# GpSimd makes the low parts of the squares, and VectorE and ScalarE share the rounding of y, in the first pass of an output stage

## The chip, the cores and the metric

One Trainium2 chip, one core, one launch. The metric is the device time of the whole kernel in microseconds. Three runs of the kernel before gave 2103.11 us in the median (2101.9 to 2104.24). All tensors lie in one core's memory; nothing is shared with other cores.

## The reference

The kernel computes two blocks in a row on a sequence of 1024 tokens with 1024 features, in float32: a gated delta net and then a block that mixes a differential attention with an mLSTM. The change lies at the seam, in the end of the first block:

```
o = rms_norm(o, norm_w) * silu(z)          # o, z: 1024 tokens x 16 heads x 128
y = o.reshape(t, 16 * 128) @ w_out         # w_out: 2048 x 1024
x = x + gate * y
x = rms_norm(x, final_g)
```

The mean in the first rms_norm is taken over the 128 features of each head.

## The kernel before

Matrix products of float32 are made from parts that TensorE multiplies fast. Each operand a is split into a high part, a rounded to the type fp32r, and a low part, a minus the high part, again rounded to fp32r. A product is three matmuls: high x high, high x low, low x high. So every operand costs one rounding copy and one subtraction on other engines before TensorE can start on it. Sums over partitions (for the norm) are products with a matrix of ones; the ones are exact, so such a sum takes two matmuls, one for the high and one for the low part.

Data lie transposed: 128 features on the partitions, 1024 tokens in the columns. A tile "of a head" is 128x1024.

The function `stage_out` computes the code above. It is written as one program for each engine, with the order of the instructions in the source and semaphores between engines; no planner orders it. The output has 8 channels of 128 features, and PSUM holds 6 banks of 512 columns for them, so the product is made in three passes over the 16 heads, with 3, 3 and 2 channels (`CH_PASS`). The list `steps` has 48 entries (pass q, head n). In the first pass (q is 0) the heads are normalised as well, and y is kept for the other passes as `y(0, n)` (high) and `y(1, n)` (low). These lie in three tensors (h_hi, m_hi, y2_hi and the same with lo), which is why the same line appears with several names in the profile. The parts of the squares, `sq_hi` and `sq_lo`, are two slots at the end of y2_hi and y2_lo, and show as y_hi and y_lo.

For head n in the first pass:

- SyncE loads o (`ob`), z (`zb`) and the rows of w_out (`m_raw`), each a few heads ahead; ob and zb have three slots, the weights two.
- ScalarE makes the square of o (L1257, into `sq`, two slots) and its high part (L1259). The subtraction that makes the low part is on VectorE (L1421, function `low_square`).
- TensorE sums the squares (L1315, L1316, four matmuls, function `sums`). The sums of head n+2 stand in the middle of head n: after the second of the three channels, which is after 12 of its 18 matmuls (L1352 to L1354).
- ScalarE turns the sums into 1/rms: two Ln from PSUM (L1272) and an Exp (L1275, `rinv`).
- VectorE multiplies z by o and by norm_w ("gated", L1414, in place in zb) and then by rinv ("mult", L1440).
- ScalarE makes the high part of y (L1279); VectorE subtracts and makes the low part (L1446). TensorE's head n waits for this low part.
- VectorE splits the weights (L1405 cast and L1407 subtraction, function `split`).

VectorE's order for head n is: mult(n), split(n), low_square(n+2), low y(n), gated(n+1). ScalarE's is: Ln(n), Exp(n), Square(n+2), high square(n+2), high y(n). GpSimd has no program in this stage; it works in the stages before and after, in element-wise products and sums (L608, L618, L627, L1742).

The second and third pass need only the weights' splits, and draining PSUM (L1382), from VectorE.

Of the kernel before, what the change touches and what calls it, by code (L numbers as in the profile page):

```python
# [22 lines left out]
F32 = mybir.dt.float32  # L23
F32R = mybir.dt.float32r
ALU = mybir.AluOpType
ACT = mybir.ActivationFunctionType
# [10 lines left out]
V_HEADS = 16  # L37
# [1105 lines left out]
def stage_out(nc, io, keep, own):  # L1143

    if True:
# [14 lines left out]
        zb = sb("zb", [P, 3, T])  # L1160
        sq = sb("sq3", [P, 2, T])
# [17 lines left out]
        def y(part, n):  # L1179

            low, middle, high = ((h_hi, next_hi, y2_hi), (h_lo, next_lo, y2_lo))[part]
            if n < KD:
                return low[:, n, :]
            return middle[:, n - KD, :] if n < KD + 2 else high[:, n - KD - 2, :]
# [52 lines left out]
        def scalar(act):  # L1237
            def squares(k):

                act.wait_ge(both_set, 5)  # L1240
                act.wait_ge(bank_used, 2 * (k + 1))
                for r in range(2):
                    if 2 <= k < KD - 1:
                        act.wait_ge(added, 2 * (k - 2) + r + 1)
                    elif k < 2:
                        act.wait_ge(ylo_done, V_HEADS)
                        act.wait_ge(ss_done, V_HEADS)
                    dst = total[:, r, :] if k == 0 else zb[:, r, :] if k == KD - 1 else sq[:, r, :]
                    nc.scalar.activation(dst, x1[:, k, :], ACT.Square,
                                         scale=(1.0 if r else both[:, k:k + 1])).then_inc(sq2, 1)  # L1250

            nc.scalar.preload_act_table_set(EXP_LN)
            def square(n):
                act.wait_ge(o_in[n % 3], 16 * (n // 3 + 1))
                if n >= 2:
                    act.wait_ge(ss_done, n - 1)
                nc.scalar.activation(sq[:, n % 2, :], ob[:, n % 3, :], ACT.Square).then_inc(sq_done, 1)  # L1257
                act.wait_ge(sq_done, n + 1)
                nc.scalar.activation(sq_hi[:, n % 2, :], sq[:, n % 2, :], ACT.Copy).then_inc(sqhi_done, 1)  # L1259

            square(0)
            square(1)
            act.wait_ge(both_set, 3)
            nc.scalar.activation(both[:], both[:], ACT.Ln).then_inc(both_set, 1)
            act.wait_ge(both_set, 4)
            nc.scalar.activation(both[:], both[:], ACT.Exp, scale=0.5).then_inc(both_set, 1)
            for n in range(V_HEADS):
                act.wait_ge(ss_done, n + 1)
                if n >= 1:
                    act.wait_ge(y_done, n)  # L1270
                for i in range(2):
                    nc.scalar.activation(rinv[:, i * HALF:(i + 1) * HALF], p_ss[i][:], ACT.Ln,  # L1272
                                         scale=1.0 / DH, bias=eps[:, 0:1]).then_inc(ln_done, 1)
                act.wait_ge(ln_done, 2 * n + 2)
                nc.scalar.activation(rinv[:], rinv[:], ACT.Exp, scale=-0.5).then_inc(rinv_done, 1)  # L1275
                if n + 2 < V_HEADS:
                    square(n + 2)
                act.wait_ge(y_done, n + 1)
                nc.scalar.activation(y(0, n), zb[:, n % 3, :], ACT.Copy).then_inc(yhi_done, 1)  # L1279
            for k in range(KD):  # L1280
                squares(k)

            act.wait_ge(ss2, 1)
            for i in range(2):
                nc.scalar.activation(rin2[:, i * HALF:(i + 1) * HALF], p_s2[i][:], ACT.Ln, scale=1.0 / D,
                                     bias=eps2[:, 0:1]).then_inc(ln2, 1)
            act.wait_ge(ln2, 2)
            nc.scalar.activation(rin2, rin2, ACT.Exp, scale=-0.5).then_inc(ri2, 1)
            for k in range(KD):
                act.wait_ge(hh, k + 1)  # L1290
                nc.scalar.activation(h_hi[:, k, :], hn[k % 3], ACT.Copy).then_inc(hhi, 1)
                if k == 1:
                    act.wait_ge(y_done, V_HEADS)
                    act.wait_ge(ss2, 2)
                    for i in range(2):
                        nc.scalar.activation(rinv[:, i * HALF:(i + 1) * HALF], p_ss[i][:], ACT.Ln, scale=1.0 / D,
                                             bias=eps[:, 0:1]).then_inc(ln2, 1)
                if k == 2:
                    act.wait_ge(ln2, 4)
                    nc.scalar.activation(rinv[:], rinv[:], ACT.Exp, scale=-0.5).then_inc(ri2, 1)  # L1300
            act.wait_ge(rt_ready, 1)
            for i in range(2):
                nc.scalar.activation(keep["rin_col"][:, 4 * i:4 * i + 4], p_ss[i][:, 0::P], ACT.Copy
                                     ).then_inc(rc_done, 1)
            act.wait_ge(x1_out, 16 * KD)
            act.wait_ge(rc_done, 2)

        def tensor(pe, next_pieces):
# [54 lines left out]
            for k in range(KD):  # L1363
# [6 lines left out]
                pe.wait_ge(hlo, k + 1)  # L1370
                next_pieces(k)

        def vector(dve, next_split):
            def drain(q):

# [40 lines left out]

            def low_square(n):
                dve.wait_ge(sqhi_done, n + 1)
                if n >= 2:
                    dve.wait_ge(ss_done, n - 1)  # L1420
                nc.vector.tensor_tensor(sq_lo[:, n % 2, :], sq[:, n % 2, :], sq_hi[:, n % 2, :].bitcast(F32),  # L1421
                                        ALU.subtract).then_inc(sqlo_done, 1)

# [11 lines left out]
            for m, (q, n) in enumerate(steps):  # L1435
                if q == 0:
                    z = zb[:, n % 3, :]
                    dve.wait_ge(gz_done, n + 1)
                    dve.wait_ge(rinv_done, n + 1)
                    nc.vector.tensor_tensor(z, z, rinv[:], ALU.mult).then_inc(y_done, 1)  # L1440
                split(m)
                if q == 0:
                    if n + 2 < V_HEADS:
                        low_square(n + 2)
                    dve.wait_ge(yhi_done, n + 1)
                    nc.vector.tensor_tensor(y(1, n), z, y(0, n).bitcast(F32), ALU.subtract).then_inc(ylo_done, 1)  # L1446
                    if n + 1 < V_HEADS:
                        gated(n + 1)
                elif n == 0:
                    drain(q - 1)  # L1450
                elif q == 2 and n % 2 and 1 <= n // 2 < first_ch[2]:
                    add_squares(n // 2)
# [17 lines left out]
            dve.wait_ge(x1_out, 16 * KD)  # L1470
            dve.wait_ge(rc_done, 2)

    return {"sync": sync, "scalar": scalar, "tensor": tensor, "vector": vector}

# [1101 lines left out]
def stage_after(nc, ctx, io, keep):  # L2578

    first, second, third = ExitStack(), ExitStack(), ExitStack()  # L2580
    with ExitStack() as front:
        for name, shape, dt in (("m_raw", [P, KD * P], F32), ("m_hi", [P, 2, KD * P], F32R),
                                ("m_lo", [P, 2, KD * P], F32R)):
            keep[name] = front.enter_context(nc.sbuf_tensor(name, shape, dt))
        with first:
            out = stage_out(nc, io, keep, first)
        with second:
            mix = stage_mix(nc, io, keep, second)
        with third:
            merge = stage_merge(nc, io, keep, third, mix)  # L2590

        with nc.Block() as block:
            @block.sync
            def _(sp):
                out["sync"](sp, lambda J: mix["load"](sp, J))
                mix["sync"](sp, merge["load"])
                merge["sync"](sp)

            @block.gpsimd
            def _(pool):  # L2600
                mix["gpsimd"](pool)

            @block.scalar
            def _(act):
                out["scalar"](act)
                mix["scalar"](act)
                merge["scalar"](act)

            @block.tensor
            def _(pe):  # L2610
                def next_pieces(k):
                    for J in range(2):
                        for h in range(2):
                            mix["piece"](pe, J, h, k)

                out["tensor"](pe, next_pieces)
                mix["tensor"](pe)
                merge["tensor"](pe)

            @block.vector  # L2620
            def _(dve):
                out["vector"](dve, lambda J: mix["split"](dve, J))
                mix["vector"](dve)
                merge["vector"](dve)
# [147 lines left out]
```

## Time and profile before

| | us |
|---|---|
| median of 3 runs | 2103.11 |
| the profiled execution's own time | 2103.15 |
| its span | 2101.4 |
| TensorE (PE) busy | 1992.7 (95%) |
| VectorE (DVE) busy | 1272.9 (61%) |
| ScalarE (ACT) busy | 853.5 (41%) |
| GpSimd (POOL) busy | 138.4 (7%) |

Busy times are sums over the instructions of an engine. Shares over the whole span hide the stages: the first pass of the output stage is about 90 of the 2101 us. Instructions of one engine overlap a little at their ends, so the step from one start to the next is somewhat shorter than the duration shown; where the text adds up an engine's work, it uses steps. Matmuls overlap more: 0.39 us long, they start 0.23 us apart.

### The profile page before, as it was taken

To read this page: it belongs to the slowest core of one execution; us is meant where nothing else is said; L and a number is where in the kernel's file an instruction comes from. 1 tells how busy PE (TensorE), PEld (TensorE's weight loads), DVE (VectorE), ACT (ScalarE), POOL (GpSimd) and SP (SyncE) were. 2 spreads that over 40 slices of the span, in tenths; PEclk is the share of its full clock that TensorE was granted. 3 is DMA by queue.
4 is the path that set the end of the run, shared out by engine and by line. 5 is a ranking of instruction groups with operands and counts; after the bars stand their busy time and mean duration, and the time that the engine had idled before them with its cause. 6 is when DMAs were issued, how large, how long until landed. Compare 5 with 4: busy or idle time off the path is not lost.

```text
span 2101.4 us, 29428 instructions
## 1 busy us (share of the span) xinstructions
PE 1992.7 (95%) x11256; PEld 1618.2 (77%) x11256; DVE 1272.9 (61%) x2415; ACT 853.5 (41%) x1376; POOL 138.4 (7%) x114
## 2 busy tenths in 40 slices
PE   4989999999999999969998999999999899999998
PEld 2667878888887878857776787777777678888877
DVE  6777777797869686749635644445353435633543
ACT  5644353544345443159403333544443337600321
POOL 0030202021111212000000000000000000000000
PEclk8999999999999999989999999999999999999999
DMA  7222233232323242548213211120312125211232
GB/s 282 86 75 70 87 89 106 65 101 71 105 68 105 67 120 68 168 158 287 80 41 136 66 60 41 41 101 21 111 41 81 61 72 219 91 49 41 85 116 80
DMA packets 128971, 200.27 MB, mean 95 GB/s; under 512 B 56596, under 2 KB 88084, under 8 KB 127808
## 3 DMA queue, kind: packets, MB, share of 16 engines
q1 hardware_dynamic: 128832, 198.39, 29.6%
q8 instruction: 91, 1.49, 0.3%
q14 instruction: 48, 0.39, 0.1%
HBM read 156.22 MB, written 42.11 MB: 94 GB/s over the span
## 4 chain that ended last, share of the span: by engine, by line
PE 47%; DVE 4%; DMA 2%; issue 2%; ACT 1%; SPq 0%; DVEq 0%; ACTq 0%
PE m_job L1682 6%; PE m_job L1684 6%; PE m_job L1683 6%; PE e_b L2369 4%; PE e_b L2371 4%; PE e_b L2370 4%; PE p_out L1352 2%; PE p_out L1353 2%; PE p_out L1354 2%; PE p_sc L1928 2%; PE p_s L1951 2%; PE e_b L2440 1%; PE e_b L2438 1%; PE e_b L2439 1%; DMA m_raw<-in_w 1%
## 5 line engine op out<-in xcount | busy, mean ns | idle before, releaser
L795 PE MATMUL p_job<-h_hi,w_hi 128*128 128x512 f32 x768 | 322.0, 419 | 18.8 <-DVE h_lo L185 17.3
L797 PE MATMUL p_job<-h_hi,w_lo 128*128 128x512 f32 x768 | 302.9, 394 | 0.0
L796 PE MATMUL p_job<-h_lo,w_hi 128*128 128x512 f32 x768 | 302.3, 394 | 0.0
L1682 PE MATMUL m_job<-h_hi,m_hi 128*128 128x512 f32 x576 | 237.6, 413 | 5.3 <-issue 4.2
L1684 PE MATMUL m_job<-h_hi,m_lo 128*128 128x512 f32 x576 | 227.4, 395 | 0.0
L1683 PE MATMUL m_job<-h_lo,m_hi 128*128 128x512 f32 x576 | 226.4, 393 | 0.0
L795 PEld LDWEIGHTS p_job<-h_hi,w_hi 128*128 128x128 f32 x768 | 146.0, 190 | 59.5 <-issue 16.2
L796 PEld LDWEIGHTS p_job<-h_lo,w_hi 128*128 128x128 f32 x768 | 146.1, 190 | 35.4 <-issue 7.9
L797 PEld LDWEIGHTS p_job<-h_hi,w_lo 128*128 128x128 f32 x768 | 145.8, 190 | 31.4
L1682 PEld LDWEIGHTS m_job<-h_hi,m_hi 128*128 128x128 f32 x576 | 108.8, 189 | 52.5 <-issue 31.0
L633 ACT ACTIVATE pre<-p_job 128x512 f32<-128x512 f32 x96 | 56.7, 591 | 179.1 <-PE p_job L797 179.1
L1684 PEld LDWEIGHTS m_job<-h_hi,m_lo 128*128 128x128 f32 x576 | 108.7, 189 | 24.6
L1683 PEld LDWEIGHTS m_job<-h_lo,m_hi 128*128 128x128 f32 x576 | 108.9, 189 | 19.6
L2369 PE MATMUL e_b<-h_hi,m_hi 128*128 128x512 f32 x256 | 99.7, 389 | 0.8 <-ACT m_gt L1747 0.8
L2371 PE MATMUL e_b<-h_hi,m_lo 128*128 128x512 f32 x256 | 99.6, 389 | 0.0
L2370 PE MATMUL e_b<-h_lo,m_hi 128*128 128x512 f32 x256 | 99.6, 389 | 0.0
L962 DVE SCALAR_TENSOR_TENSOR qv<-pre,conv_w,qv 128x1024 f32<-128x1024 f32 x72 | 93.3, 1296 | 5.2 <-ACT qv L638 3.5
L1084 DVE TENSOR_TENSOR UL<-UL,lane_tmp 64x31 f32<-64x31 f32 (+15 forms) x248 | 83.0, 335 | 8.5
L1081 DVE TENSOR_TENSOR lane_tmp<-UL,AL 64x31 f32<-64x31 f32 (+15 forms) x248 | 82.8, 334 | 7.5
L1669 DVE CAST m_hi<-m_raw 128x1024 fp32r<-128x1024 f32 x38 | 26.2, 691 | 92.0 <-DMA m_raw<-in_w 80.3
L608 POOL TENSOR_TENSOR gam<-gam,tri 128x512 f32<-128x512 f32 x32 | 41.7, 1302 | 515.3 <-DVE gam L1019 515.3
L1126 DVE SCALAR_TENSOR_TENSOR S<-S,gl,p_head 128x128 f32<-128x128 f32 x128 | 38.9, 345 | 52.0 <-PE p_head L929 52.0
(395 smaller groups left out, 4166.3 us busy)
## 6 DMA issues: line engine op xcount, KB each, us to landing
w_raw<-in_w SPq DMA_DIRECT2D x49, 512.0 KB
m_raw<-in_w SPq DMA_DIRECT2D x49, 512.0 KB, 3.8
rows<-grows SPq DMA_DIRECT2D x32, 512.0 KB, 6.6
ada<-in_ada_w SPq DMA_DIRECT2D x8, 1024.0 KB, 5.3
z_scr<-pre SPq DMA_DIRECT2D x16, 512.0 KB, 2.6
o_scr<-oT SPq DMA_DIRECT2D x64, 128.0 KB, 1.8
ob<-o_scr SPq DMA_DIRECT2D x16, 512.0 KB, 4.8
zb<-z_scr SPq DMA_DIRECT2D x16, 512.0 KB, 4.8
```

The source lines that it names most:

```text
L795: nc.tensor.matmul(bank, hi, h_hi[:, k, cut], start=(k == 0), stop=False)
L796: nc.tensor.matmul(bank, hi, h_lo[:, k, cut], start=False, stop=False)
L797: last = nc.tensor.matmul(bank, lo, h_hi[:, k, cut], start=False, stop=(k == KD - 1))
L962: nc.vector.scalar_tensor_tensor(dst, pre[:, job(i, j) % 2, q:q + T], w, dst, ALU.mult, ALU.add).then_inc(conv_step, 1)
L1081: nc.vector.tensor_tensor(step, bc(UL[0:LANES, 0:r, j], 2, w), bc(AL[0:LANES, j, r:], 1, r), ALU.mult).then_inc(lane_done, 1)
L1084: nc.vector.tensor_tensor(UL[0:LANES, 0:r, r:], UL[0:LANES, 0:r, r:], step, ALU.subtract).then_inc(lane_done, 1)
L1682: nc.tensor.matmul(bank, hi, h_hi[:, k, cut], start=(k == 0), stop=False)
L1683: nc.tensor.matmul(bank, hi, h_lo[:, k, cut], start=False, stop=False)
L1684: last = nc.tensor.matmul(bank, lo, h_hi[:, k, cut], start=False, stop=(k == KD - 1))
L2369: nc.tensor.matmul(bank, hi, hi_rhs, start=first, stop=False)
L2370: nc.tensor.matmul(bank, hi, lo_rhs, start=False, stop=False)
L2371: return nc.tensor.matmul(bank, lo, hi_rhs, start=False, stop=final)
```

## The change

From head 2 on the low part of the squares is made by GpSimd, with the same subtraction. GpSimd waits for the high square, for its own instruction of the head before, and for the sums that read the slot last. ScalarE waits, before it writes a slot of `sq`, for the low square that reads it. VectorE keeps the low squares of heads 0 and 1. The high part of y is made by ScalarE for even heads as before, and by VectorE, with a copy, for odd heads. The kernel has a new GpSimd program for this stage, which runs ahead of the one that the next stage has.

```diff
@@ ScalarE, square(n)
                 if n >= 2:
                     act.wait_ge(ss_done, n - 1)
+                    act.wait_ge(sqlo_done, n - 1)
                 nc.scalar.activation(sq[:, n % 2, :], ob[:, n % 3, :], ACT.Square).then_inc(sq_done, 1)
@@ ScalarE, loop over the heads
                 if n + 2 < V_HEADS:
                     square(n + 2)
-                act.wait_ge(y_done, n + 1)
-                nc.scalar.activation(y(0, n), zb[:, n % 3, :], ACT.Copy).then_inc(yhi_done, 1)
+                if n % 2 == 0:
+                    act.wait_ge(y_done, n + 1)
+                    nc.scalar.activation(y(0, n), zb[:, n % 3, :], ACT.Copy).then_inc(yhi_done, 1)
@@ GpSimd, new
+        def gpsimd(pool):
+            for n in range(2, V_HEADS):
+                pool.wait_ge(sqlo_done, n)
+                pool.wait_ge(sqhi_done, n + 1)
+                pool.wait_ge(ss_done, n - 1)
+                nc.gpsimd.tensor_tensor(sq_lo[:, n % 2, :], sq[:, n % 2, :], sq_hi[:, n % 2, :].bitcast(F32),
+                                        ALU.subtract).then_inc(sqlo_done, 1)
@@ VectorE, low_square(n), now called for n = 0 and 1 only
                 dve.wait_ge(sqhi_done, n + 1)
-                if n >= 2:
-                    dve.wait_ge(ss_done, n - 1)
                 nc.vector.tensor_tensor(sq_lo[:, n % 2, :], sq[:, n % 2, :], sq_hi[:, n % 2, :].bitcast(F32),
                                         ALU.subtract).then_inc(sqlo_done, 1)
@@ VectorE, loop over the steps
                 if q == 0:
-                    if n + 2 < V_HEADS:
-                        low_square(n + 2)
+                    if n % 2:
+                        dve.wait_ge(y_done, n + 1)
+                        nc.vector.tensor_copy(y(0, n), z).then_inc(yhi_done, 1)
                     dve.wait_ge(yhi_done, n + 1)
```

## Rows read from the trace of the kernel before

**Rows 1.** Windows: busy us (instructions) by engine, granted clock, DMA share, GB/s
```profile
core 0: us, PE busy (x) PEld busy (x) DVE busy (x) ACT busy (x) POOL busy (x), PEclk, DMA share, GB/s
930.00:1020.00 90.00, 82.19 (x330) 62.98 (x330) 84.32 (x93) 80.04 (x91) 0.00 (x0) 0.94 0.70 235
1024.00:1070.00 46.00, 45.06 (x199) 36.87 (x198) 14.06 (x28) 4.09 (x4) 0.00 (x0) 1.00 0.16 47
```

**Rows 2.** Timeline of VectorE, one head: start us, us, instruction, idle before
```profile
961.57 1.23 DVE L1440 TENSOR_TENSOR zb<-zb,rinv 128x1024 f32<-128x1024 f32 x1
962.71 0.35 DVE L1405 CAST wo_hi<-m_raw 128x384 fp32r<-128x384 f32 x1
963.10 0.56 DVE L1407 TENSOR_TENSOR wo_lo<-m_raw,wo_hi 128x384 fp32r<-128x384 f32 x1
963.57 1.22 DVE L1421 TENSOR_TENSOR y_lo<-sq,y_hi 128x1024 fp32r<-128x1024 f32 x1
964.71 1.22 DVE L1446 TENSOR_TENSOR h_lo<-zb,h_hi 128x1024 fp32r<-128x1024 f32 x1
965.84 1.28 DVE L1414 SCALAR_TENSOR_TENSOR zb<-ob,nw,zb 128x1024 f32<-128x1024 f32 x1
967.15 1.22 DVE L1440 TENSOR_TENSOR zb<-zb,rinv 128x1024 f32<-128x1024 f32 x1
```

**Rows 3.** Timeline of ScalarE around the same head
```profile
964.35 1.27 ACT L1272 ACTIVATE rinv<-p_ss,eps 128x512 f32<-128x512 f32 x2 [0.19 <-PE p_ss L1316]
...
967.92 1.06 ACT L1259 ACTIVATE y_hi<-sq 128x1024 fp32r<-128x1024 f32 x1
968.89 1.05 ACT L1279 ACTIVATE h_hi<-zb 128x1024 fp32r<-128x1024 f32 x1
```

**Rows 4.** Timeline of PE, first and last matmul of a head and the next
```profile
960.39 0.50 PE L1352 MATMUL p_out<-h_hi,wo_hi 128*128 128x512 f32 x1 [0.27 <-DVE h_lo L1446]
...
965.28 0.39 PE L1354 MATMUL p_out<-h_hi,wo_lo 128*128 128x512 f32 x1
965.98 0.50 PE L1352 MATMUL p_out<-h_hi,wo_hi 128*128 128x512 f32 x1 [0.31 <-DVE h_lo L1446]
```

**Rows 5.** GpSimd's groups, busy us and mean ns; one by line, min/median/max ns
```profile
L618 POOL TENSOR_TENSOR at<-gam,rows 128x256 f32<-128x256 f32 x64 | 45.8, 737 | 158.2 <-ACT gam L730 158.2
L627 POOL TENSOR_TENSOR qd<-qd,qv 128x2048 f32<-128x2048 f32 x8 | 36.8, 4602 | 36.2 <-ACT qd L746 36.2
L1742 POOL TENSOR_TENSOR qw<-qw,qb x4: 2382/2764/3344, 1249.3 to 1622.0; 128x1024 f32<-128x1024 f32 x4
```

**Rows 6.** By line, window 1375 to 1380 us: min/median/max ns
```profile
L2067 DVE SCALAR_TENSOR_TENSOR dm<-m_rows,m_cols,m_tri x8: 339/340/2468, 1375.4 to 1379.4; 128x128 f32<-128x128 f32 x8
```

**Rows 7.** Timeline of VectorE and GpSimd just before
```profile
1374.30 1.23 DVE L1671 TENSOR_TENSOR m_lo<-m_raw,m_hi 128x1024 fp32r<-128x1024 f32 x1
1374.42 3.34 POOL L1742 TENSOR_TENSOR qw<-qw,qb 128x1024 f32<-128x1024 f32 x1 [122.68 <-ACT qw L1815]
```

**Rows 8.** Timeline of VectorE and GpSimd in an earlier stage
```profile
243.29 4.61 POOL L627 TENSOR_TENSOR qd<-qd,qv 128x2048 f32<-128x2048 f32 x1 [4.69 <-ACT qd L746]
243.47 4.98 DVE L942 CAST w_hi<-w_raw 128x1024 fp32r<-128x1024 f32 x1
```

**Rows 9.** By line, min/median/max ns of a cast of 1024 columns
```profile
L1669 DVE CAST m_hi<-m_raw x38: 681/693/696, 1137.4 to 1717.2; 128x1024 fp32r<-128x1024 f32 x38
```

**Rows 10.** Timeline of VectorE at head 2 and in head 14
```profile
944.79 1.23 DVE L1440 TENSOR_TENSOR zb<-zb,rinv 128x1024 f32<-128x1024 f32 x1 [1.96 <-ACT rinv L1275]
...
1011.87 1.23 DVE L1440 TENSOR_TENSOR zb<-zb,rinv 128x1024 f32<-128x1024 f32 x1
...
1014.23 1.22 DVE L1446 TENSOR_TENSOR y_lo<-zb,y_hi 128x1024 fp32r<-128x1024 f32 x1 [0.26 <-ACT y_hi L1279]
```

**Rows 11.** Windows where PE's granted clock is low, and before
```profile
1197.50:1199.30 1.80, 0.99 (x16) 0.99 (x16) 1.70 (x6) 0.60 (x1) 0.00 (x0) 1.00 0.04 7
1200.00:1204.00 4.00, 4.00 (x12) 3.17 (x11) 0.13 (x1) 0.00 (x0) 0.00 (x0) 0.57 0.53 162
936.00:941.00 5.00, 4.90 (x12) 3.85 (x13) 4.93 (x7) 3.76 (x4) 0.00 (x0) 0.51 0.69 227
```

More of the change, by code:

```diff
@@ L1471, in vector @@
             dve.wait_ge(rc_done, 2)
-    return {"sync": sync, "scalar": scalar, "tensor": tensor, "vector": vector}
+    return {"sync": sync, "gpsimd": gpsimd, "scalar": scalar, "tensor": tensor, "vector": vector}
 MIX_INPUTS = ("qa", "ka", "va", "qb", "kb", "vb")
@@ L2600, in _ @@
             def _(pool):
+                out["gpsimd"](pool)
                 mix["gpsimd"](pool)
```

## The prediction

> **What bounds the kernel now.** I read the page first (the span, and the profiled execution's own time of 2103.15 us, against 2103.11 us for the median of the runs shown: the same, so sums made on the trace carry over without a correction). Then the windows of the stretch that the change touches. The first pass of the output stage runs from about 930 to 1020 us, and in it three engines are nearly full at once: PE 82.2, VectorE 84.3 and ScalarE 80.0 us of 90, GpSimd 0.0 [rows 1]. After 1024 us PE alone is full (45.1 of 46 us) and VectorE has 14.1 us. So time lost or won in the first pass is not made up later: the following stretch is PE's.
>
> The timeline of one head shows who sets the pace. On VectorE the starts are: mult 961.57, cast of w 962.71, low part of w 963.10, low square 963.57, low part of y 964.71, gated 965.84, next mult 967.15 [rows 2]. The steps are 1.14 + 0.39 + 0.47 + 1.14 + 1.13 + 1.31 = 5.58 us, with no idle time printed: VectorE is the bound, one head per 5.58 us. ScalarE does two Ln, Exp, Square, Copy and the Copy that makes the high y; its row after Ln had waited 0.19 us for PE [rows 3], so it has little slack. PE starts a head at 960.39 and its last matmul at 965.28, 21 steps of 0.233 us, and starts the next head at 965.98 after 0.31 us of waiting for the low y [rows 4]. PE's work is 22 matmuls (18 for the head, 4 sums) x 0.233 = 5.1 us, so PE has about 0.5 us of slack per head.
>
> **The change part by part.**
>
> *Low squares off VectorE.* 14 instructions of 1.14 us (heads 2 to 15, issued in heads 0 to 13) go from VectorE: -1.14 us per head.
>
> *Low squares onto GpSimd.* The trace has a GpSimd tensor_tensor of the same size (128x1024, two SBUF inputs): four, shortest 2.38 us [rows 5]. The others give 737 / 256 = 2.88 and 4602 / 2048 = 2.25 ns per column, hence 2.30 to 2.95 us for 1024. Rounding on the write to fp32r is not in any GpSimd row, so I keep 2.95 us as the top and take 2.38 us. Its own time is not what it costs: it starts when ScalarE's high square is done, and its reader is PE's sums(n+2), 12 matmuls into head n. The high square ends at 967.92 + 1.06 = 968.98 [rows 3]; it is the one of head k+4 if PE's head at 960.39 is k, so its sums come 12 matmuls (2.8 us) into PE's head k+2, which starts at 965.98 + 5.58 = 971.6: at 974.4. 2.4 us from 968.98 fits. Nothing is queued behind it on GpSimd. ScalarE's new wait (low square n-2 done) is already implied by its earlier wait for the sums.
>
> *What GpSimd does to VectorE.* This is the term that decides. Eight equal 128x128 scalar_tensor_tensor take 340 ns each (median), but one of them, beside GpSimd's 128x1024 product, takes 2468 ns [rows 6]. The delay is 2.47 - 0.34 = 2.13 us, against 2.38 us of GpSimd work. The order is visible too: GpSimd's instruction started at 1374.42 during a VectorE tensor_tensor that ran from 1374.30 to 1375.53, and took 3.34 us, 0.96 longer than 2.38; the run of eight began then, and its one long instruction is the price on VectorE's side [rows 7]. So one waits for the other to end, in both directions. A VectorE cast that started at 243.47, beside a GpSimd product of 4.61 us from 243.29, took 4.98 us [rows 8], where one of this size alone takes 0.69 [rows 9]: it ended at 248.45, 0.55 us after GpSimd did. All VectorE instructions of a head (mult, both w parts, low y, gated, the new cast) are casts or have two SBUF inputs, the kinds held in these rows. Bounds: 0 us (no hold at all) to 2.95 us; between the row's 2.13 and 2.38 I take 2.2 us per head.
>
> The Trainium skill, page "SBUF — State Buffer", section "Who interferes with whom", says that GpSimd and a VectorE instruction with two SBUF inputs use a common read port as an exclusive lock, and the later one blocks fully. By it the hold would be GpSimd's whole 2.38 us, 0.18 us more per head, some 2.5 us more in all than my sum; the 2.13 us row is a little short of it.
>
> *Rounding y.* In odd heads a VectorE copy of 128x1024 to fp32r replaces ScalarE's: 0.693 us by the median of the cast's row, 0.73 us with the step to the next dependent instruction (as 0.39 to 0.35 for the small cast). The copy also waits for mult, which lies 0.86 us of w work before it: no stall. ScalarE loses 1.05 us in odd heads, which buys nothing as long as VectorE is the bound. In even heads the low y follows ScalarE's Copy: without the low square between them, VectorE idles. Head 14 shows that today: mult 1011.87, low y 1014.23 with 0.26 us of waiting, 2.36 us after mult instead of the 2.00 us of w work alone [rows 10]. So an even head gets up to 0.36 us of idle time, in which the hold by GpSimd may fall.
>
> Even head: 5.58 - 1.14 + 2.2 + (0 to 0.36) = 6.64 to 7.00, that is +1.06 to +1.42 us. Odd head: 5.58 - 1.14 + 0.73 + 2.2 = 7.37, that is +1.79 us. Heads 2 to 13 are six of each: 6 x (1.06 to 1.42) + 6 x 1.79 = 17.1 to 19.3, middle 18.2 us. Heads 0 and 1 would add 1.2 (an even head) + 1.8, but VectorE idles 1.96 us before the mult of head 2 today, released by ScalarE's rinv [rows 10], behind sums that follow the low y of head 0. That chain moves by head 0's 1.2 us only, so the two heads cost 1.2 us. Head 14 costs nothing. Head 15 hangs on sums(15), in PE's head 13: mult, then w work 0.86 and a cast 0.73 instead of a wait of 0.36 on ScalarE: +0.35 us. Sum: 18.2 + 1.2 + 0.35 = 19.8 us.
>
> *TensorE's clock.* With a head in 7.0 to 7.4 us PE has 5.1 us of work and stops once per head for about 2 us. Such a stop is in the trace: from 1197.5 to 1199.3 PE runs 16 tiny transposes (0.99 us busy, still at full clock), and from 1200 to 1204 the granted clock is 0.57, that is mostly the 1.2 GHz level, with 12 matmuls in 4 us [rows 11] instead of 4 / 0.233 = 17. One such stretch costs PE 5 x 0.233 = 1.2 us, which the 2 us of new slack takes up, except at the end of the pass, where PE's lag is carried on. I add 1.0 us (0 to 1.2).
>
> Total: +20.8 us. 2103.15 + 20.8 = 2124.0 us. DMA is no term: the loads get 1.5 us more per head.
>
> **Rivals.**
>
> A. *No hold.* If GpSimd's and VectorE's work really lie side by side, VectorE needs 4.44 + 0.36 us in even and 5.17 us in odd heads, and the loop through sums decides. For even heads: PE's start 960.39, Ln 964.35, then Exp, Square, high square (to 968.98), Copy of y from 968.89 to 969.94 [rows 3, 4], low y 1.2 us: about 971.2, two heads in 10.85 us, 5.43 per head. Gain 14 x 0.15 = 2.2 us: 2100.9 us. This is the case on the other side, not slower; it comes when the hold per head falls below the 0.6 us or so that the edit takes off VectorE (5.58 - 4.80 in even heads, 5.58 - 5.17 in odd). For it: GpSimd and ScalarE have room. Against it: two places of the trace, two kinds of instruction [rows 6 to 8].
>
> B. *GpSimd's write to fp32r is slow*, 2.95 us, and the hold with it: 0.75 us more in each of 13 heads (the second is absorbed): +9.8 us, 2133.8 us. For it: no row of GpSimd writes fp32r. Against it: the rate falls with size (2.88 ns at 256 columns, 2.33 at 1024, 2.25 at 2048), so the top of the range belongs to small instructions.
>
> C. *The clock falls and stays down.* From 936 to 941 us, at a clock of 0.51, PE ran 12 matmuls in 5 us [rows 11], 0.42 each: 22 are 9.2 us per head, 2.0 us more than VectorE's 7.2: 14 x 2.0 = 28 us more, 2152 us. For it: the stop at 1197.5. Against it: at 9.2 us a head PE has no idle time, and after 1024 us, where PE is full, the clock is 1.00 [rows 1], so it would rise again; a partial form costs 3 to 8 us.
>
> **How the numbers follow.** The forecast (held by 2.1 to 2.4 us per head): 0.76. A: 0.09. B: 0.09. C: 0.06. About 0.2%, 4.2 us, is what a measurement of this kernel can tell from no change; A's 2.2 us lies within it. So slower 0.91, same 0.07, faster 0.02. The forecast's own range: a hold of 2.0 us gives 13 x 0.2 = 2.6 us less, full cover in the even heads 1.1 and no loss of clock 1.0 less; a hold of 2.38 gives 2.3 us more, no cover 1.1 and the clock 0.2 more: 2119 to 2128. The range reaches down to a GpSimd instruction that falls partly into idle time, and up to B and the partial form of C: 2115 to 2134.
>
> **What would show it.** In the changed trace: GpSimd has 14 low squares, some longer than 2.38 us because they wait for VectorE; in each head one VectorE instruction is 2.1 to 2.4 us longer than its kind; mult to mult is about 6.8 us in even and 7.4 us in odd heads; PE waits about 2 us per head for the low y; before 915 us nothing changes, and after the pass only the offset. Wrong would be the forecast if VectorE's mean times stay at 1.22 and 1.28 us (A), if GpSimd's shortest low square is near 3 us (B), or if PE is full and its clock is 0.5 through the pass (C).

## The result: 0.87% slower, as forecast

| | before | after |
|---|---|---|
| median, us | 2103.68 (2101.9 to 2106.33, 4 runs) | 2122.02 (2117.75 to 2124.32, 4 runs) |
| ratio, 95% interval | | 1.0087 (1.0072 to 1.0103) |
| span of the profiled execution | 2101.4 | 2121.0 |
| GpSimd busy | 138.4 | 177.0 |
| VectorE busy | 1272.9 | 1292.0 |

The forecast was 2124.0 us with a range of 2115 to 2134. VectorE gave 14 instructions of 1.22 us away and took eight casts of 0.69, and its busy time rose by 19.1 us: its other instructions got longer.

The windows of the kernel after (same columns as [rows 1]). In the first 90 us PE does 70.2 instead of 82.2 us of work, and VectorE is no less full than before (86.8 against 84.3 us):

```profile
core 0: us, PE busy (x) PEld busy (x) DVE busy (x) ACT busy (x) POOL busy (x), PEclk, DMA share, GB/s
930.00:1020.00 90.00, 70.15 (x265) 53.35 (x265) 86.82 (x70) 61.79 (x71) 36.05 (x13) 0.89 0.64 215
1045.00:1090.00 45.00, 44.70 (x197) 36.92 (x198) 13.46 (x28) 4.09 (x4) 0.00 (x0) 1.00 0.17 49
```

The timeline of VectorE for two heads of the kernel after answers to [rows 2]; the first head is odd, the second even:

```profile
979.38 1.23 DVE L1448 TENSOR_TENSOR zb<-zb,rinv 128x1024 f32<-128x1024 f32 x1
980.52 2.56 DVE L1415 CAST wo_hi<-m_raw 128x384 fp32r<-128x384 f32 x1
983.12 0.56 DVE L1417 TENSOR_TENSOR wo_lo<-m_raw,wo_hi 128x384 fp32r<-128x384 f32 x1
983.59 0.69 DVE L1453 CAST h_hi<-zb 128x1024 fp32r<-128x1024 f32 x1
984.31 1.23 DVE L1455 TENSOR_TENSOR h_lo<-zb,h_hi 128x1024 fp32r<-128x1024 f32 x1
985.46 1.28 DVE L1424 SCALAR_TENSOR_TENSOR zb<-ob,nw,zb 128x1024 f32<-128x1024 f32 x1
986.77 1.23 DVE L1448 TENSOR_TENSOR zb<-zb,rinv 128x1024 f32<-128x1024 f32 x1
987.91 2.54 DVE L1415 CAST wo_hi<-m_raw 128x384 fp32r<-128x384 f32 x1
990.48 0.56 DVE L1417 TENSOR_TENSOR wo_lo<-m_raw,wo_hi 128x384 fp32r<-128x384 f32 x1
990.96 1.22 DVE L1455 TENSOR_TENSOR m_lo<-zb,m_hi 128x1024 fp32r<-128x1024 f32 x1
```

One instruction of each of the heads 0 to 13 is too long. Here it is the small cast, 2.56 us where it is 0.35 when nothing holds it. The difference, 2.21 us, is what this text calls a hold. From mult to mult the odd head takes 986.77 - 979.38 = 7.39 us, against 5.58 before. GpSimd's own rows (after) say when it worked and for how long, by the timeline and by line (min/median/max ns):

```profile
980.04 2.82 POOL L1380 TENSOR_TENSOR y_lo<-sq,y_hi 128x1024 fp32r<-128x1024 f32 x1 [3.84 <-ACT y_hi L1260]
```
```profile
L1380 POOL TENSOR_TENSOR y_lo<-sq,y_hi x14: 2342/2820/3458, 932.3 to 1024.0; 128x1024 fp32r<-128x1024 f32 x14
```

It starts at 980.04 inside VectorE's mult, which ends at 980.61, and runs to 982.86; VectorE's cast ends at 983.08. Its 2.82 us are 0.48 more than the shortest, 2.34, and 980.04 + 0.48 is 980.52, the start of the cast. So each waits for the other in turn: GpSimd for the end of mult, then the cast for GpSimd. The hold moves about: in other heads it is on the cast of y, the low y, or mult.

From here on I compare "the pass": from the start of the first Square on ScalarE to the start of the first drain of PSUM on VectorE. That leaves out where the pass starts, which differs between profiled executions (918.6 to 923.4 us in the ones below, latest in the kernel before). Before: 923.4 to 1025.2 = 101.8 us. After: 921.6 to 1044.4 = 122.8 us, +21.0. What follows the pass took 1076.2 and 1076.6 us: nothing is given back. The kernel before has one trace, so every difference of a pass below is taken against its 101.8 us.

### The profile page after: what moved, and what is told of

Same layout as the page of the kernel before. It is cut to its first block, busy times and chain, and to the rows that moved or that the text cites. A ratio compares the mean times of both kernels' runs of the same rounds, so it can differ in the third digit from the quotient of the medians.

```text
span 2121.0 us, 29428 instructions
## 1 busy us (share of the span) xinstructions
PE 2000.0 (94%) x11256; PEld 1624.0 (77%) x11256; DVE 1292.0 (61%) x2409; ACT 846.2 (40%) x1368; POOL 177.0 (8%) x128
## 4 chain that ended last, share of the span: by engine, by line
PE 49%; DVE 4%; issue 1%; ACT 1%; DMA 1%; SPq 0%; DVEq 0%; ACTq 0%
PE m_job L1691 6%; PE m_job L1693 6%; PE m_job L1692 6%; PE e_b L2378 4%; PE e_b L2380 4%; PE e_b L2379 4%; PE p_out L1354 2%; PE p_out L1355 2%; PE p_out L1356 2%; PE p_sc L1937 2%; PE p_s L1960 2%; PE e_b L2449 1%; PE e_b L2448 1%; PE e_b L2447 1%; PE p_t L1949 1%
```

## The experiments

The theory (H) is that of the prediction: GpSimd's two-input instruction holds VectorE for about 2.2 us, VectorE's time sets the pass, and VectorE is freed of 1.14 us and held for 2.2. Rivals: R1, the cost is the rounding of y on VectorE; R2, the sums come later because GpSimd is slow and far down the chain. Each kernel is timed against the kernel before on the same chip.

| kernel | time, us (kernel before, timed beside it) | ratio (95%) | pass, us |
|---|---|---|---|
| low squares on GpSimd only | 2113.59 (2101.64) | 1.0054 (1.0037 to 1.0071) | 115.3 |
| rounding of y only | 2106.63 (2101.64) | 1.0017 (1.0007 to 1.0028) | 106.4 |
| extra subtraction, one tile | 2122.13 (2101.64) | 1.0094 (1.0079 to 1.0109) | 121.6 |
| extra subtraction, own operands | 2124.83 (2101.63) | 1.0109 (1.0094 to 1.0124) | 126.4 |
| extra copy | 2109.68 (2100.54) | 1.0043 (1.0028 to 1.0058) | 110.2 |
| extra memset | 2101.35 (2100.54) | 1.0003 (0.9993 to 1.0013) | 101.2 |
| half the columns on GpSimd | 2113.97 (2100.54) | 1.0063 (1.0046 to 1.0080) | 112.7 |
| plain float32 sums | 2103.01 (2101.64) | 1.0008 (0.9999 to 1.0017) | 103.4 |
| high squares only | 2087.61 (2101.63) | 0.9930 (0.9914 to 0.9947) | 91.8 |

The change of the time and that of the pass agree within 1.5 us, except for half the columns (+13.4 and +10.9), the high squares only (-14.0 and -10.0) and the whole change (+18.3 and +21.0). A pass comes from one execution, a time from a median.

### The two halves of the change

Low squares on GpSimd, ScalarE rounds y in all heads:

```diff
-                if n % 2 == 0:
-                    act.wait_ge(y_done, n + 1)
-                    nc.scalar.activation(y(0, n), zb[:, n % 3, :], ACT.Copy).then_inc(yhi_done, 1)
+                act.wait_ge(y_done, n + 1)
+                nc.scalar.activation(y(0, n), zb[:, n % 3, :], ACT.Copy).then_inc(yhi_done, 1)
...
-                    if n % 2:
-                        dve.wait_ge(y_done, n + 1)
-                        nc.vector.tensor_copy(y(0, n), z).then_inc(yhi_done, 1)
```

> One half of the change: GpSimd makes the low squares, ScalarE still rounds y in every head. Theory H (GpSimd's instruction holds VectorE for 2.2 us per head): every head from 2 to 13 is an even head of the prediction, +1.06 to +1.42 us, 14.9 us in the middle, +1.2 for heads 0 and 1, +1 for the clock: about 17 us over the kernel before, 2119 to 2122 us. Rival R1 (the cost is VectorE's rounding of y, GpSimd is nearly free): within 2 us of the kernel before, 2102 to 2106 us.

Measured 12 us over the kernel before, less than expected, and well outside R1. Its timeline of VectorE has a period of 6.67 us, the lower end (6.64) of the prediction's even head:

```profile
957.59 1.23 DVE L1447 TENSOR_TENSOR zb<-zb,rinv 128x1024 f32<-128x1024 f32 x1
958.73 2.57 DVE L1414 CAST wo_hi<-m_raw 128x384 fp32r<-128x384 f32 x1
961.33 0.56 DVE L1416 TENSOR_TENSOR wo_lo<-m_raw,wo_hi 128x384 fp32r<-128x384 f32 x1
961.81 1.22 DVE L1451 TENSOR_TENSOR h_lo<-zb,h_hi 128x1024 fp32r<-128x1024 f32 x1
962.95 1.28 DVE L1423 SCALAR_TENSOR_TENSOR zb<-ob,nw,zb 128x1024 f32<-128x1024 f32 x1
964.26 1.23 DVE L1447 TENSOR_TENSOR zb<-zb,rinv 128x1024 f32<-128x1024 f32 x1
```

The low y comes right after the weights with no idle time: while GpSimd holds the cast, ScalarE's rounding of y goes on, so the 0.36 us of waiting is covered. The pass is 13.5 us longer, of which 12.8 lie between the mults of head 2 and head 14, 1.06 per head. The expectation had 14.9 there, 1.2 for heads 0 and 1 and 1.0 for the clock; the last two came out as 0.8 and nothing.

The other half, on the kernel before:

```diff
-                act.wait_ge(y_done, n + 1)
-                nc.scalar.activation(y(0, n), zb[:, n % 3, :], ACT.Copy).then_inc(yhi_done, 1)
+                if n % 2 == 0:
+                    act.wait_ge(y_done, n + 1)
+                    nc.scalar.activation(y(0, n), zb[:, n % 3, :], ACT.Copy).then_inc(yhi_done, 1)
...
+                    if n % 2:
+                        dve.wait_ge(y_done, n + 1)
+                        nc.vector.tensor_copy(y(0, n), z).then_inc(yhi_done, 1)
                     dve.wait_ge(yhi_done, n + 1)
```

> The other half: VectorE rounds y for odd heads, VectorE keeps all low squares, GpSimd has no work here. Theory H: 0.73 us in each of the six odd heads 3 to 13, head 1's share vanishes in the idle time before head 2, +0.35 us in head 15: +4.7 us, 2108 to 2109 us. R1: nearly all of the 18 us, about 2120 us.

Measured +5.0 us, and the pass 4.6 us longer, where the prediction's terms say 4.7. R1 is out. The two halves together give 13.5 + 4.6 = 18.1 us of pass; the whole change costs 21.0. The remaining 2.9 us appear only with both. By the starts of mult in the three traces, 0.5 us of them lie in heads 0 and 1, 0.6 in heads 2 to 13, and 1.6 between head 14 and head 15. The last two are a loss of TensorE's clock that neither half has (see the section on the prediction).

### An instruction that nobody waits for

The kernel before, with a GpSimd instruction added in heads 0 to 11. It writes a slot of y2_lo that is not in use until head 13 (`dum`). In head 13 VectorE waits for the last of them, which has been over for more than 10 us by then:

```diff
+        def gpsimd(pool):
+            nc.gpsimd.memset(dum, 0.0).then_inc(dum_done, 1)
+            for n in range(2, V_HEADS - 2):
+                pool.wait_ge(dum_done, n - 1)
+                pool.wait_ge(sqhi_done, n + 1)
+                nc.gpsimd.tensor_tensor(y2_lo[:, 3, :], dum, dum, ALU.subtract).then_inc(dum_done, 1)
```

> The kernel before, and beside it GpSimd subtracts a 128x1024 tile from itself (two SBUF reads, write to fp32r) in heads 0 to 11, started by the high square as in the changed kernel; nothing reads the result, nothing waits for it but VectorE in head 13. VectorE keeps all its own work. Theory H: 12 holds of 2.2 us less the 1.96 us of idle time before head 2: +24 us, about 2128 us, and in each head one VectorE instruction longer by 2.1 to 2.2 us. Rival R2 (the changed kernel loses because the sums wait for GpSimd, not because VectorE is held): no change, 2102 to 2106 us.

Its pass is 19.8 us longer. R2 falls: no consumer waits for the result, and the time is lost all the same. The size was off, because this instruction is shorter than the real one: 12 x 1.70 less 1.96 is 18.4 us, and 1.3 more are lost in head 12, where mult waited 1.30 us for rinv behind matmuls at TensorE's low clock. By line and by the timeline (VectorE's mult to mult is 7.29 us, the hold 2.05 - 0.35 = 1.70):

```profile
L1379 POOL TENSOR_TENSOR y_lo<-y_lo x12: 1896/2910/2958, 933.2 to 1011.3; 128x1024 fp32r<-128x1024 f32 x12
```
```profile
967.55 1.22 DVE L1448 TENSOR_TENSOR zb<-zb,rinv 128x1024 f32<-128x1024 f32 x1
968.69 2.05 DVE L1413 CAST wo_hi<-m_raw 128x384 fp32r<-128x384 f32 x1
...
974.84 1.22 DVE L1448 TENSOR_TENSOR zb<-zb,rinv 128x1024 f32<-128x1024 f32 x1
...
1025.41 1.23 DVE L1448 TENSOR_TENSOR zb<-zb,rinv 128x1024 f32<-128x1024 f32 x1 [1.30 <-ACT rinv L1276]
```
```profile
1018.90:1022.30 3.40, 3.40 (x10) 2.64 (x9) 3.37 (x5) 1.06 (x1) 0.00 (x0) 0.51 0.87 298
```

The same with the operands of the changed kernel (and ScalarE's wait for them):

```diff
-                nc.gpsimd.tensor_tensor(y2_lo[:, 3, :], dum, dum, ALU.subtract).then_inc(dum_done, 1)
+                nc.gpsimd.tensor_tensor(y2_lo[:, 3, :], sq[:, n % 2, :], sq_hi[:, n % 2, :].bitcast(F32),
+                                        ALU.subtract).then_inc(dum_done, 1)
```

> As the run with the extra subtraction, but GpSimd reads the two tiles that it reads in the changed kernel (the square and its high part) in place of one tile twice; that run's instruction took 1.90 us at the shortest and held VectorE 1.70 us, the changed kernel's 2.37 and 2.2. If reading two different tiles is what makes it 2.4 us long, each head's hold is 2.2 us and a head 7.8 us: the pass is 12 x 2.2 less 1.96 = 24 us longer than before, about 2126 us. If the length has another cause (what waits for it, the stage), the pass stays near +20 us, 2122 us.

The pass is 24.6 us longer, where 24 was expected, and the hold is 2.63 - 0.56 = 2.07 us. The agreement is in part luck: 12 x 2.07 less 1.96 is 22.9, and head 12 again took 1.1 us more, 6.73 for 5.59, with a wait of its next mult for rinv. The hold and its cause don't depend on that:

```profile
L1381 POOL TENSOR_TENSOR y_lo<-sq,y_hi x12: 2455/2574/3366, 933.0 to 1017.0; 128x1024 fp32r<-128x1024 f32 x12
```
```profile
963.61 2.63 DVE L1418 TENSOR_TENSOR wo_lo<-m_raw,wo_hi 128x384 fp32r<-128x384 f32 x1
```

So one tile read twice takes 1.90 us and two different tiles 2.46 at the shortest, and the hold follows. In this kernel VectorE keeps its low squares and a head takes 7.66 us, in the run with GpSimd alone it doesn't and a head takes 6.67. The difference is 0.99 us, with a hold that is 0.15 longer (2.22 for 2.07): the 1.14 us that VectorE was freed of were won in full, and lost again to the hold.

### Which GpSimd instruction holds VectorE

```diff
-                nc.gpsimd.tensor_tensor(y2_lo[:, 3, :], dum, dum, ALU.subtract).then_inc(dum_done, 1)
+                nc.gpsimd.memset(dum, 0.0).then_inc(dum_done, 1)
```

> As the run with the extra subtraction, but GpSimd only fills the tile with zeros (memset 128x1024, a write and no SBUF read, 0.96 us in the trace before). It starts when the high square is done, when VectorE is in the low part of w or the low square (two SBUF inputs each). Theory H1 (what is contended is a read port, and two-input instructions are held only by a GpSimd instruction that reads): no change, 2102 to 2106 us, and VectorE's tensor_tensors keep 1.22 us. Rival H2 (any GpSimd instruction holds any VectorE instruction): 12 x 0.9 less 2 us, +9 us, about 2113 us. The Trainium skill, page SBUF - State Buffer, section Who interferes with whom, states H1.

No change. The timelines of both engines show a memset that lies wholly beside a VectorE instruction with two inputs, and neither is longer for it. All twelve memsets fell beside such instructions and none beside a cast, so whether a memset holds a cast is not tested.

```profile
964.31 1.22 DVE L1429 TENSOR_TENSOR y_lo<-sq,y_hi 128x1024 fp32r<-128x1024 f32 x1
```
```profile
964.32 0.95 POOL L1379 MEMSET y_lo<- 128x1024 f32 x1 [4.73 <-ACT y_hi L1260]
```

```diff
-                nc.gpsimd.tensor_tensor(y2_lo[:, 3, :], dum, dum, ALU.subtract).then_inc(dum_done, 1)
+                nc.gpsimd.tensor_copy(y2_lo[:, 3, :], dum).then_inc(dum_done, 1)
```

> As above with a GpSimd copy of the tile to fp32r (one SBUF read and one write). H1 and H2 both say held; the length is open, between the memset's 0.95 us and the subtraction's 2.38: 12 x (0.9 to 2.2) less 2 us, +9 to +24 us, 2113 to 2128 us. If two inputs on both sides were needed for a hold: no change, about 2104 us.

One read is enough. The copy takes 1.08 us at the shortest. In ten of the twelve heads the small cast takes 1.20 instead of 0.35 us (a hold of 0.85), and in two it is the low y, with two inputs: 2.06 for 1.22. 12 x 0.85 less 1.96 is 8.2 us; the pass is 8.4 us longer:

```profile
L1379 POOL CAST y_lo<-y_lo x12: 1081/1242/2061, 929.3 to 999.2; 128x1024 fp32r<-128x1024 f32 x12
```
```profile
967.28 1.20 DVE L1413 CAST wo_hi<-m_raw 128x384 fp32r<-128x384 f32 x1
```
```profile
929.34 2.05 POOL L1379 CAST y_lo<-y_lo 128x1024 fp32r<-128x1024 f32 x1 [12.99 <-ACT y_hi L1260]
930.41 2.06 DVE L1456 TENSOR_TENSOR h_lo<-zb,h_hi 128x1024 fp32r<-128x1024 f32 x1
```

### Half the columns

```diff
-                nc.gpsimd.tensor_tensor(sq_lo[:, n % 2, :], ...
+                nc.gpsimd.tensor_tensor(sq_lo[:, n % 2, 0:HALF], ...
...
+                    if n + 2 < V_HEADS:
+                        dve.wait_ge(sqhi_done, n + 3)
+                        dve.wait_ge(ss_done, n + 1)
+                        nc.vector.tensor_tensor(sq_lo[:, n % 2, HALF:T], sq[:, n % 2, HALF:T],
+                                                sq_hi[:, n % 2, HALF:T].bitcast(F32), ALU.subtract).then_inc(half_done, 1)
```

PE waits for both parts, and ScalarE before it writes the slot again.

> The changed kernel with the low square cut in two: GpSimd makes 512 columns (1.27 us by its row of that size, hold about 1.1 us), VectorE the other 512 (0.6 us step). Theory H (each column on GpSimd costs VectorE twice what it costs VectorE to do it): even heads 5.58 - 1.14 + 0.6 + 1.1 = +0.56, odd heads +1.29, 12 heads +11.1, heads 0, 1 and 15 +1, clock +1: +13 us, about 2117 us. Rival (sharing the columns balances the engines and wins): below 2110 us.

Measured +13.4 us, and 10.9 us of pass; the expected +13 agrees with the time and not with the pass, and the 2.5 us between the two are not explained. The hold is 1.53 - 0.56 = 0.97 us for 512 columns, and 1.46 - 0.35 = 1.11 where it falls on the small cast, about half of the hold for 1024. An even head takes 6.16 us, against 5.59 with no columns on GpSimd and 6.83 with all. From these three points I infer that no share of the columns balances the engines; other shares were not run.

```profile
963.53 1.53 DVE L1422 TENSOR_TENSOR wo_lo<-m_raw,wo_hi 128x384 fp32r<-128x384 f32 x1
```

### Is VectorE's time what the pass costs?

This kernel takes the low squares off VectorE without GpSimd, with sums in plain float32:

```diff
-                act.wait_ge(sq_done, n + 1)
-                nc.scalar.activation(sq_hi[:, n % 2, :], sq[:, n % 2, :], ACT.Copy).then_inc(sqhi_done, 1)
...
-                    nc.tensor.matmul(p_ss[i][:], ones_r[:], sq_hi[:, n % 2, cut], start=True, stop=False)
-                    last = nc.tensor.matmul(p_ss[i][:], ones_r[:], sq_lo[:, n % 2, cut], start=False, stop=True)
+                    last = nc.tensor.matmul(p_ss[i][:], ones[:], sq[:, n % 2, cut], start=True, stop=True)
```

> The kernel before without high and low squares: PE multiplies the float32 square by the float32 ones (2 matmuls per head instead of 4), as the last norm of this stage does already, where the matmuls start 0.43 us apart. VectorE loses 1.14 us, ScalarE 1.06 us per head, GpSimd does nothing. Theory H (VectorE's time is what the pass costs, and 1.14 us of it is all that the change was after): the bound passes to PE, 18 x 0.233 + 2 x 0.43 = 5.05 us per head and 0.1 to 0.2 of waits, against 5.58: 13 x 0.35 to 0.45 = 4.5 to 6 us gained, 2097.5 to 2099.5 us. Rival (PE or the loop through the sums bounds already, and VectorE's load is a symptom): 2102 us or more.

No gain. I had misread the rows of the last norm: a float32 matmul leaves two records, 0.43 us apart, so it takes 0.86 us (at a granted clock of 1.00). The records of the sums are 64 for 32 instructions, and their timeline on PE has four for a head's two:

```profile
L1314 PE MATMUL p_ss<-sq,ones x64: 592/592/1222, 923.1 to 1013.2; 128*128 128x512 f32 x64
```
```profile
965.12 1.88 PE L1314 MATMUL p_ss<-sq,ones 128*128 128x512 f32 x4
966.43 0.80 PE L1350 MATMUL p_out<-h_hi,wo_hi 128*128 128x512 f32 x1
```

PE then has 18 x 0.233 + 1.7 = 5.9 us per head, and the heads follow each other every 5.86 us with VectorE 69.9 of 90 us busy. The bound went to PE, and the run says nothing of what VectorE's 1.14 us are worth. The next one says more. It leaves out the low parts of the squares: the sum is of squares rounded to fp32r, written so by ScalarE. In both kernels SyncE's load of o waits in addition for the square that reads the slot.

```diff
-                nc.scalar.activation(sq[:, n % 2, :], ob[:, n % 3, :], ACT.Square).then_inc(sq_done, 1)
+                nc.scalar.activation(sq_hi[:, n % 2, :], ob[:, n % 3, :], ACT.Square).then_inc(sq_done, 1)
...
-                    last = nc.tensor.matmul(p_ss[i][:], ones[:], sq[:, n % 2, cut], start=True, stop=True)
+                    last = nc.tensor.matmul(p_ss[i][:], ones_r[:], sq_hi[:, n % 2, cut], start=True, stop=True)
```

> The low parts of the squares are left out: ScalarE writes the square rounded to fp32r at once, PE sums it with 2 fast matmuls per head, VectorE and GpSimd make nothing of it. Per head VectorE 4.44 us and 0.26 to 0.36 of idle time, ScalarE 4.4, PE 20 x 0.233 = 4.7. Theory H (VectorE's own time sets the pass, 5.58 us per head, so that the 1.14 us that the change took off it would have been worth most of itself, had they not come back as a hold): 4.8 to 5.0 us per head, 13 x 0.6 to 0.8 = 8 to 10 us gained, 2091 to 2094 us. Rival (the loop through the sums bounds near 5.4 us whatever VectorE does): at most 2.5 us gained, 2099 us or more.

Measured 14.0 us less than before, more than expected. The pass is 918.6 to 1010.4 = 91.8 us, 10.0 shorter, the upper end of the expectation; the other 4 us are not explained. Its pass started 4.8 us earlier than that of the kernel before. But that of the memset run started 4.2 us earlier too: its profiled execution took 2098.84 us, and its median was no lower than that of the kernel before. Mult follows mult in 4.81 us where nothing else waits, and VectorE and ScalarE idle a little, for a load of o and for each other:

```profile
973.16 1.23 DVE L1436 TENSOR_TENSOR zb<-zb,rinv 128x1024 f32<-128x1024 f32 x1
977.97 1.23 DVE L1436 TENSOR_TENSOR zb<-zb,rinv 128x1024 f32<-128x1024 f32 x1
```

This kernel beats both, at the price of the precision of the norm's sum. It removes work from three engines at once, so its gain isn't VectorE's alone. It shortens the loop through the sums too, by the high square, so it doesn't test whether that loop, with the high square in it, would bound at 5.4 us. That stays open; at 5.58 us and more per head VectorE bounds.

## Why the prediction was right, step by step

From mult(0), 930.19 us, to the first drain, 1044.40, the kernel after takes 114.2 us, the kernel before 93.5 (931.68 to 1025.22). The 20.7 us split by the starts of mult:

| stretch | before | after | difference | predicted |
|---|---|---|---|---|
| mult(0) to mult(2) | 13.11 | 14.08 | +0.97 | +1.2 |
| mult(2) to mult(14), 12 heads | 67.08 | 84.86 | +17.78 | +18.2 |
| mult(14) to mult(15) | 5.29 | 6.85 | +1.56 | 0, and 1.0 for the clock |
| mult(15) to the drain | 8.06 | 8.42 | +0.36 | +0.35 |

- **Heads 0 and 1.** 0.97 for 1.2 us, but by another path. The forecast had mult(2) wait for rinv as before. In the kernel after it waits for nothing, and VectorE's own 6.72 + 7.36 = 14.08 us set it:

```profile
944.27 1.23 DVE L1448 TENSOR_TENSOR zb<-zb,rinv 128x1024 f32<-128x1024 f32 x1
```
- **The hold.** Taken as 2.2 us; measured 2.06 to 2.21 in the twelve heads in which VectorE had not been idle before it (1.36 and 1.77 in heads 0 and 2), 2.07 in the run with the same operands. The Trainium skill's rule (page "SBUF — State Buffer", section "Who interferes with whom") that the later one blocks fully is borne out in who holds whom, and in that a memset does not hold a two-input instruction (1.22 us) while a reading copy does (2.06 for 1.22). The prediction draws on it for VectorE instructions with two inputs. The casts that were held have one; the runs show their hold, 2.56 us for 0.35, and not its reason. The rule's literal size, GpSimd's whole instruction, is 2.34 to 2.46 us at the shortest here, and the hold was 0.1 to 0.4 us less.
- **Even and odd heads.** Odd heads took 7.32 us in the mean (7.24 to 7.40), forecast 7.37. Even heads 6.83 (6.65 to 7.01), forecast 6.64 to 7.00. In head 6, at 6.66, the hold fell on the cast of the weights, and ScalarE rounded y meanwhile; in head 4, at 7.01, it fell on mult, in front of ScalarE's rounding, and the wait came on top. Heads 8 and 12, at 6.86 and 6.87, lie in the range by luck: the wait for y was covered, and 0.26 us came from a wait for rinv that the sum doesn't have (see the clock below).
- **GpSimd's write to fp32r** (rival B). Its shortest is 2.34 us, no slower than the float32 rows [rows 5]: B is out.
- **No hold** (rival A). Out by the longer instructions in every run with a reading GpSimd instruction.
- **The clock.** The mechanism was as forecast, the size was not. PE had stood still for 2.19 us when it started head 13. At the low level its first eight matmuls took 3.51 us, where eight steps of 0.233 are 1.86: 1.65 us for the stretch, not 1.2. sums(15) lie behind them, and with them Ln, Exp and mult(15), which idled 2.08 us for rinv, 1.56 us more of the pass where the forecast had 1.0:

```profile
1027.96 0.79 PE L1354 MATMUL p_out<-y_hi,wo_hi 128*128 128x512 f32 x1 [2.19 <-DVE y_lo L1455]
1028.55 0.63 PE L1355 MATMUL p_out<-y_lo,wo_hi 128*128 128x512 f32 x1
```
```profile
987.10:990.50 3.40, 3.40 (x9) 2.67 (x8) 3.37 (x3) 1.06 (x1) 3.13 (x1) 0.51 0.91 308
1028.00:1032.00 4.00, 4.00 (x11) 3.19 (x12) 3.67 (x5) 1.06 (x1) 0.00 (x0) 0.58 0.00 0
```
```profile
1035.98 1.23 DVE L1448 TENSOR_TENSOR zb<-zb,rinv 128x1024 f32<-128x1024 f32 x1 [2.08 <-ACT rinv L1276]
```

The same happened in PE's heads 7, 9 and 11 (the first row of the windows is head 7), and PE's slack did not take all of it up. Behind head 7 Ln waited 2.08 us for the sums and the next mult 0.26 us for rinv; mult(13), behind head 11, waited 0.26 us as well:

```profile
991.17 1.27 ACT L1273 ACTIVATE rinv<-p_ss,eps 128x512 f32<-128x512 f32 x2 [2.08 <-PE p_ss L1318]
993.63 1.23 DVE L1448 TENSOR_TENSOR zb<-zb,rinv 128x1024 f32<-128x1024 f32 x1 [0.26 <-ACT rinv L1276]
```

So the clock cost 1.56 + 2 x 0.26 = 2.1 us in all. The runs with the extra subtraction show the loss too: where GpSimd's work ends, in head 12, the slack is gone. In the run with GpSimd alone PE stopped for 1.2 to 1.8 us per head, the granted clock stayed at 1.00 from head 2 on (the row below), and mult(14) to mult(15) took 5.25 us, with no such loss:

```profile
945.00:1037.00 92.00, 74.73 (x314) 57.45 (x312) 85.29 (x71) 68.28 (x76) 32.64 (x12) 1.00 0.62 203
```

Rival C, a clock that stays down, did not come: the granted clock over the 90 us was 0.89, against 0.94 before.
- **The whole.** Two sizes were off and cancelled. Without the two waits of 0.26 us, heads 2 to 13 cost 17.3 us for the 18.2 of the forecast, and the clock cost 2.1 for 1.0. That the stretches add up to 20.7 for 20.8 is in part luck; the terms that carry the forecast, the hold and VectorE's time per head, were each within 0.15 us. The medians differ by 18.3 us (interval 15 to 22), the passes of the two profiled executions by 21.0. The kernel before's median was 2100.5 to 2103.7 us in four series of runs, and where the pass starts varied by up to 4.8 us between profiled executions; so the sum of 20.8 and the 18.3 of the medians can't be told apart.

## What to carry to other kernels

Before work goes from VectorE to GpSimd, look for a place in the trace where a GpSimd instruction that reads SBUF runs beside VectorE's casts or two-input instructions, and read the price there: VectorE's longest instruction less its usual time. If VectorE is the bound and its instructions are of these kinds, most of GpSimd's time becomes VectorE's (0.8 to 0.9 of it here), and a subtraction that takes VectorE 1.14 us takes 2.2 of it when GpSimd does it. Work that is moved within a full stage has to be priced on the engine that is full; leaving it out, on all engines, was what made this pass shorter.

## What the runs showed of the hardware that was not expected

- A GpSimd subtraction of 128x1024 takes 1.90 us when both operands are the same tile, and 2.34 to 2.46 us with two tiles, each at the shortest.
- A GpSimd memset of 0.95 us beside a two-input VectorE instruction costs neither anything; a GpSimd copy of 1.08 us holds a cast for 0.85 us and a two-input instruction for 0.84.
- GpSimd gets its turn when VectorE's running instruction ends, though VectorE's instructions follow each other without a gap: the one that started at 980.04 took 0.48 us more than the shortest, as long as mult still ran.
- In the kernel after, PE stopped for 1.96 to 2.19 us before its heads 7, 9, 11 and 13, and some eight matmuls of each ran at the low level (granted clock 0.50 to 0.51). Heads 3 and 5, after stops of 2.07 and 2.09 us, ran at the full one, and so did every head from 2 on of the run with GpSimd alone, whose stops were 1.2 to 1.8 us.
- A matmul of float32 with 512 columns is two records, 0.43 us apart, at full clock: 0.86 us against 0.23 for fp32r. A sum by high and low parts is two matmuls of 0.23, cheaper on PE than one in float32.
